# Thirteen weight blocks of a transformer stage formed by single-pass products, with GpSimd making their low parts

## The reference

```python
h = rms_norm_2(x, norm1_g[l]) * (1 + sc1) + sh1
proj = h @ w_in[l]                                   # 1024 -> 7168
ca, cb, q, k, v, gate_conv, gate_attn = jnp.split(proj, offsets, axis=-1)
y_conv = conformer_conv(ca, cb, conv_dw[l], ...)     # u = a*sigmoid(b); 31 taps per channel; layer norm; silu; @ w_pw2
y_attn = diff_attention(q, k, v, cos, sin, ...)      # rms norm of q and k per map, rope, 16 maps, softmax
merged = jax.nn.sigmoid(gate_conv) * y_conv + jax.nn.sigmoid(gate_attn) * y_attn
x = x + g1 * (merged @ w_out[l])
```

## Time and profile before

| | |
|---|---|
| median of 3 runs | 1594.1 us (1593.49 to 1595.61) |
| the profiled execution's own time | 1594.08 us |
| its span in the trace | 1592.4 us |
| mean granted TensorE clock | 0.985 |
| PE, DVE, ACT, POOL busy | 1518.2, 736.5, 490.1, 45.3 us |

### The profile page before, as it was taken

The page is one execution under the profiler, slowest core; times in us unless marked ns, Lnnn a source line. Parts: engine busy times, 40 slices in busy tenths (PEclk is TensorE's granted clock), DMA queues, the critical chain, the costliest instruction groups (busy, mean ns, idle before and its releaser), DMA issues.

```text
span 1592.4 us, 27380 instructions
## 1 busy us (share of the span) xinstructions
PE 1518.2 (95%) x10546; PEld 1015.8 (64%) x10546; DVE 736.5 (46%) x1245; ACT 490.1 (31%) x758; POOL 45.3 (3%) x97
## 2 busy tenths in 40 slices
PE   6999999999999899999999999988989999989988
PEld 6999968757697799997854455463434444444442
DVE  5555447255665565555499855461211221222212
ACT  4433343152443443334001262032222222222221
POOL 6000010100000000001000000000000000000000
PEclk9999999999999999999999999998999999999999
DMA  9855384221346475637644433419997997988984
GB/s 321 287 169 181 136 299 142 89 98 54 124 155 231 146 257 165 210 127 256 204 145 142 171 102 112 170 53 403 348 402 297 360 349 257 346 342 313 352 333 167
DMA packets 156217, 350.92 MB, mean 220 GB/s; under 512 B 12655, under 2 KB 57919, under 8 KB 155712
## 3 DMA queue, kind: packets, MB, share of 16 engines
q1 hardware_dynamic: 152464, 343.05, 59.6%
q0 software_dynamic: 1792, 3.09, 0.7%
q10 hardware_dynamic: 1840, 3.17, 0.5%
HBM read 579.89 MB, written 2.16 MB: 366 GB/s over the span
## 4 chain that ended last, share of the span: by engine, by line
PE 71%; DVE 12%; DMA 8%; SPq 3%; ACT 3%; issue 2%; DVEq 0%; ACTq 0%
PE bank L675 16%; PE bank L2879 8%; PE bank L654 8%; PE bank L2907 6%; DVE arena L2356 6%; PE bank L2157 5%; PE bank L1078 4%; DMA ring<-in_w_exp_down 4%; DMA ring<-in_w_exp_gu 3%; PE bank L2809 3%; PE bank L1814 3%; PE bank L2789 3%; PE bank L1831 2%; SPq L3147 2%; PE bank L1087 2%
## 5 line engine op out<-in xcount | busy, mean ns | idle before, releaser
L675 PE MATMUL bank<-x_high,w_high 128*128 128x256 f32 x704 | 201.1, 286 | 6.1 <-DVEq L252 6.1
L675 PE MATMUL bank<-x_low,w_high 128*128 128x256 f32 x704 | 200.7, 285 | 0.0
L675 PE MATMUL bank<-x_high,w_low 128*128 128x256 f32 x704 | 199.5, 283 | 0.0
L747 DVE TENSOR_TENSOR w_low<-ring,w_high 128x2048 fp32r<-128x2048 f32 x60 | 137.4, 2292 | 76.8 <-ACT w_high L712 76.6
L2157 PE MATMUL bank<-ring,xT 128*128 128x512 f32 x384 | 166.0, 593 | 1.8 <-ACT arena L2514 1.8
L675 PEld LDWEIGHTS bank<-x_high,w_high 128*128 128x128 f32 x704 | 134.0, 190 | 7.6 <-issue 6.9
L675 PEld LDWEIGHTS bank<-x_high,w_low 128*128 128x128 f32 x704 | 135.5, 192 | 0.0
L675 PEld LDWEIGHTS bank<-x_low,w_high 128*128 128x128 f32 x704 | 134.2, 191 | 0.7
L712 ACT ACTIVATE w_high<-ring 128x2048 fp32r<-128x2048 f32 x60 | 114.6, 1913 | 60.4 <-PE bank L654 59.2
L2157 PEld LDWEIGHTS bank<-ring,xT 128*128 128x128 f32 x384 | 72.6, 190 | 91.9 <-issue 91.8
L2907 PE MATMUL bank<-ring,arena 128*32 128x512 f32 x1024 | 118.7, 605 | 7.9 <-DMA ring<-in_w_exp_down 7.9
(11 more groups left out here) (573 smaller groups left out, 2418.8 us busy)
## 6 DMA issues: line engine op xcount, KB each, us to landing
ring<-in_w_exp_gu SPq DMA_DIRECT2D x512, 512.0 KB
ring<-in_w_exp_down SPq DMA_DIRECT2D x128, 1024.0 KB
ring<-in_w_in SPq DMA_DIRECT2D x42, 768.0 KB, 6.1
ring<-in_ffn_w_gate SPq DMA_DIRECT2D x22, 1024.0 KB, 5.8
ring<-in_ffn_w_up SPq DMA_DIRECT2D x22, 1024.0 KB, 8.6
ring<-in_ffn_w_down SPq DMA_DIRECT2D x21, 1024.0 KB, 10.1
ring<-in_w_ada SPq DMA_DIRECT2D x24, 768.0 KB, 5.7
ring<-in_w_in SPq DMA_DIRECT2D x21, 512.0 KB, 7.9
```

Source lines behind the costliest of these rows:

```text
L675: ins = pe.eng.matmul(bank[:, k * S:(k + 1) * S], ff_w[f][w][:, c, k, :], (x_high, x_low)[x][:, c, :], start=c == 0 and i == 0, stop=c == ...
L747: v.eng.tensor_tensor(low[:], raw_piece((base + a) % NS, p), high[:].bitcast(F32), ALU.subtract).then_inc(low_set[p], 1)
```

## The change

Block 0 stays as it was. Blocks 1 to 13 are formed by the three single-pass products, each block in two halves, so there are 26 halves (numbered 0 to 25, block 1 has halves 0 and 1). ScalarE makes all 26 high parts; VectorE makes the low parts of halves 0 and 1, GpSimd those of the other 24. (`BY_VEC` is 2.) High parts rotate over three places in the ring's tails (the last one has its own), so half k is cut after TensorE has left half k-3. The stage's input is cut too: `x_high` and `x_rest`, and again in place after block 0.

The convolution is as it was: its running sum stays in SBUF, and its instructions and operands are unchanged (L2417 in the new file).

Along with it: the squares of q and k are formed and summed on ScalarE (`map_squares`: 64 instructions of 128x64 with an accumulated sum) where VectorE had four of 128x2048; q's norm is applied later, as a scale in the exponentials; both gains are folded on the part that isn't turned; the rope runs over q and k together (12 instructions instead of 24); the convolution's transposes of the second half come after block 11 instead of block 9; the gates' store to DRAM has a place of its own, and VectorE waits for it ahead of the copies of q.

```diff
+            for half in cut_halves[BY_VEC:]:
+                eng.wait_ge(half_high, half.number)
+                eng.tensor_tensor(half.low, half.cut(wide[half.block % NS], half.k),
+                                  half.high.bitcast(F32), ALU.subtract).then_inc(pool_low, 1)
...
+            for k in range(26):
+                block = 1 + k // 2
+                cut_halves.append(Half(first + block,
+                                       by_columns if block < 4 else by_rows, k % 2,
+                                       places[k % 3] if k < 25 else last_place,
+                                       cut_halves[k - 3] if 3 <= k < 25 else None))
...
+            def half_parts(half):
+                k = cut_halves.index(half)
+                if k < BY_VEC:
+                    return pe_half(pe, half)
+                wait(pool_low, k + 1 - BY_VEC)
+                return half.high, half.low
...
+            def split_projected(to, block, x_parts):
+                banks = [to.fill() for _ in range(T)]
+                for m, half in enumerate(cut_halves[2 * block - 2:2 * block]):
+                    high, low = half_parts(half)
+                    for t, b in enumerate(banks):
+                        for c in range(4):
+                            for i, (w, x) in enumerate(PAIRS):
+                                ins = mm(ps[b][:], x_parts[x][:, 4 * m + c, t * P:(t + 1) * P],
+                                         (high, low)[w][:, c, :], start=m == c == i == 0,
+                                         stop=m == 1 and c == 3 and i == 2, skip_group_check=True)
+                        if m:
+                            ins.then_inc(to.full, 1)
+                    half.left_by = (to.full, to.n - (0 if m else T - 1))
...
-            for _ in range(4):
-                projected(to_act)
+            for block in range(4, 8):
+                split_projected(to_act, block, x_parts)
             conv_to_tokens(0)
-            for _ in range(2):
-                projected(to_act)
+            for block in range(8, 12):
+                split_projected(to_act, block, x_parts)
             conv_to_tokens(1)
-            for _ in range(2):
-                projected(to_act)
             wait(qk_ready, 1)
...
+            wait(x_high_now, IN_XN)
+            tt(x_rest[0], xT[:], x_high[:].bitcast(F32), ALU.subtract).then_inc(x_parts_set, 1)
+            for half in cut_halves[:BY_VEC]:
+                vec_half(v, half)
...
-                do(tt(sq, qk[:, at], qk[:, at], ALU.mult))
-                do(e.tensor_reduce(ss[:, at], sq, AX.X, ALU.add))
...
+            def map_squares(i, n, t):
+                for m in range(n * 8, (n + 1) * 8):
+                    ins = f(squares[:, i * T + t, m], qk[:, i * T + t, m], ACT.Square,
+                            accum_out=ss[:, i * T + t, m:m + 1])
+                do(ins)
```

More of the change, by code:

```diff
@@ L2152, in features @@
                 release.append((to.full, to.n))
+            first = pe.block
+            places = [ring_tail[(first + i) % NS] for i in range(3)]
+            x_rest.append(ring_tail[(first + 3) % NS][:].rearrange("p (c s) -> p c s", c=DC))
+            for k in range(26):
[4 more added lines that the diff above has]
+                                       cut_halves[k - 3] if 3 <= k < 25 else None))
@@ new lines, in half_parts, with split_features @@
+            def half_parts(half):
[4 more added lines that the diff above has]
+                return half.high, half.low
+            def split_features(to, block, x_parts):
+                for half in cut_halves[2 * block - 2:2 * block]:
+                    b = to.fill()
+                    high, low = half_parts(half)
+                    for k in range(2):
+                        for c in range(DC):
+                            at = slice(k * P, (k + 1) * P)
+                            for i, (w, x) in enumerate(PAIRS):
+                                ins = mm(ps[b][:, k * S:(k + 1) * S], (high, low)[w][:, c, at],
+                                         x_parts[x][:, c, :], start=c == i == 0,
+                                         stop=c == DC - 1 and i == 2, skip_group_check=True)
+                    ins.then_inc(to.full, 1)
+                    half.left_by = (to.full, to.n)
+                pe.block += 1
+                release.append((to.full, to.n))
@@ L2230, in pe_part @@
             features(to_vec)
-            features(to_act)
+            wait(x_parts_set, OF_HYBRID)
+            split_features(to_act, 1, (x_high, x_rest[0]))
             wait(taps_loaded, 64)
@@ L2367, in vec_part @@
             wait(qk_set, 1)
-            for i in range(2):
-                at = slice(i * T, (i + 1) * T)
-                do(tt(sq, qk[:, at], qk[:, at], ALU.mult))
-                do(e.tensor_reduce(ss[:, at], sq, AX.X, ALU.add))
-            v.ask()
+            do(e.reciprocal(ss, ss))
+            for t in range(T):
+                x = qk[:, T + t]
+                do(tt(x, x, along(ss[:, T + t], HD), ALU.mult))
+                do(tt(x, x, every(kg, MAPS), ALU.mult))
+            for t in range(T):
+                turned = qk[:, t, :, 0:ROT]
+                do(tt(turned, turned, every(qg[:, 0:ROT], MAPS), ALU.mult))
             wait(convT_set, 4)
@@ L2376, in vec_part @@
             v.ask()
[L2377 to L2386, removed]
+            for t in range(T):
+                both = qk[:, t::T]
+                sin, cos = (trig[:, j, t].unsqueeze(1).unsqueeze(1).to_broadcast([P, 2, MAPS, 8])
+                            for j in range(2))
+                at = slice(2 * t, 2 * t + 2)
+                x1, x2 = both[:, :, :, 0:8], both[:, :, :, 8:16]
+                do(tt(rot_a[:, at], x1, sin, ALU.mult))
+                do(tt(rot_b[:, at], x2, sin, ALU.mult))
                 do(tt(x1, x1, cos, ALU.mult))
                 do(tt(x2, x2, cos, ALU.mult))
-                do(tt(x1, x1, rot_b[:, i], ALU.subtract))
-                do(tt(x2, x2, rot_a[:, i], ALU.add))
+                do(tt(x1, x1, rot_b[:, at], ALU.subtract))
+                do(tt(x2, x2, rot_a[:, at], ALU.add))
             e.sem_inc(qk_ready, 1)
+            do(ts(ss[:, 0:T], ss[:, 0:T], HD ** -0.5, None, ALU.mult))
             v.answer()
@@ L2397, in vec_part @@
             e.sem_inc(ln_ready, 1)
+            wait(gate_stored, 32)
             for c in range(0, HEADS, 2):
@@ L2505, in act_part @@
             act_to_features(a, xT, DC, modT[:, 0], modT[:, 1])
+            a.taken()
+            f(x_high[:], xT[:], ACT.Copy).then_inc(x_high_now, 1)
+            for half in cut_halves[0:3]:
+                act_half(a, half)
             a.get()
@@ L2514, in evict, with conv_gate @@
                 do(f(dst, src, how, **more), act_free)
-            for c in range(0, DC, 2):
+            def conv_gate(c):
                 b = mine.take()
@@ L2520, in act_part, with qk_columns @@
                 do.count[act_free.name] = do.count.get(act_free.name, 0) + 1
[L2521 to L2526, removed]
+            def qk_columns(i, n, t):
+                b = mine.take()
+                evict(qk[:, i * T + t, n * 8:(n + 1) * 8, :], view(ps[b], 0, (8, HD)))
+            def map_squares(i, n, t):
[3 more added lines that the diff above has]
+                do(ins)
+            wait(vec_full, 2)
+            wait(x_parts_set, OF_HYBRID)
+            f(x_again[:], xT[:], ACT.Copy).then_inc(x_high_now, 1)
+            conv_gate(0)
+            act_half(a, cut_halves[3])
+            conv_gate(2)
+            for half in cut_halves[4:7]:
+                act_half(a, half)
+            conv_gate(4)
+            act_half(a, cut_halves[7])
+            conv_gate(6)
+            act_half(a, cut_halves[8])
             def conv_tokens(half):
```

104 lines of the change are left out of this document (76 added, 28 removed).

## The result

The changed kernel takes 1677.76 us (median of 4, 1676.35 to 1678.73) beside 1594.7 for the kernel before on the same chip: ratio 1.0526 [1.051, 1.0541], 83 us slower.

What follows compares the result with a forecast made beforehand. Up to 919 us two full queues, TensorE's blocks and VectorE's convolution, bound it. Exclusion moves the convolution's end to 977 and the mask from 928.0 to 996.5: 1594.1 + 68.5 = 1662.6, said as 1662, range 1612 to 1682.

Steps and rivals of the forecast that it cites:

- T: End of the whole convolution on VectorE: forecast at 977 us, from 879.05 + 0.6 + 21 x 4.6 + 1.
- the way from T to the mask: VectorE's norms, passes over k, rope, layer norm and copies between convolution and masked scores: 19.5 us, mask at 996.5.
- TensorE's part: Single-pass products in blocks 1 to 13: 11.52 us a features block, 10.98 a projected one, saving 36.1 us.
- the side-by-side rival: GpSimd's subtractions and VectorE's convolution run together: T = 880, mask at 904, -24 us, 1570; chance 0.08.
- GpSimd's price: One 128x2048 low-part subtraction on GpSimd: 4.6 us, the middle of 4.1 and 5.1.
- Exclusion: Convolution taps and GpSimd subtractions, each reading two SBUF tiles, exclude each other, so their times add: 21 x 4.6 us.
- Exclusion, GpSimd getting its turns: Main case: beside the convolution GpSimd's subtractions each get a turn; 1645 to 1680 us, chance 0.55.
- VectorE holding: Rival: VectorE never lets GpSimd in during the convolution, halves stay 47.5 us, mask at 990, 1656; chance 0.22.
- the rival's sign: Mark of the rival with VectorE holding: TensorE waits for low parts, not for the convolution (`conv_ready`).
- my "1 us" for it: ScalarE's high parts waiting behind bank copies in its queue, blocks 4 to 9: full, not over; counted 1 us.
- Late start of block 1: Block 1 on TensorE waits for two of VectorE's three 2.29 us subtractions: taken as 2 us.
- Behind the mask: Softmax chain on VectorE and ScalarE taken as unchanged; blocks 12 and 13 save 5.8 us in shadow: counted 0.

Runs made afterwards that it cites:

- experiment 9: Experiment 8's kernel with ScalarE's exponential and sine ahead of block 1's high parts, and half 2's high part behind the copy of x: 1578.64 us, 0.9909.
- experiment 3: Kernel before the change plus eight unneeded 128x2048 subtractions on GpSimd beside the convolution's first half: 1630.9 us in one run.
- Experiment 1: Changed kernel with the convolution's running sum in PSUM banks until the last tap, so most taps read one SBUF tile: 1598.7 us, 1.0031.
- experiment 10: Experiment 9's kernel with the convolution's running sum put back in SBUF: 1664.07 us, 1.0453.
- experiments 5 and 6: Kernel before plus unneeded GpSimd subtractions parted by one or two memsets beside the convolution: 1631.37 us; the same with VectorE draining before each tap: 1638.39 us.
- Experiment 2: Changed kernel with VectorE waiting for its own last instruction before the first of each tap's four: 1678.29 us, 1.0522.
- experiment 8: Experiment 1's kernel with GpSimd starting half 22 only behind the passes over k (after the layer norm): 1591.45 us, 0.9986.

## Why the prediction was right, and where its sizes were off

The sign, and the reason for it, were right: 1677.8 measured, 1662 forecast, range 1612 to 1682. The total was 15.8 us short. Two of its terms, T and the way from T to the mask, were each off by more than twice that and nearly cancelled: the mask came 5.2 us later than forecast. Nearly all of the rest is the 5.9 and 4.4 us behind it.

**TensorE's part: right.** 96 products in 11.50 us, four projected blocks in 43.55 and 43.80 (10.9 each, 10.98 forecast); the side-by-side rival's mask at 904, 2 us ahead of what experiment 9 reached once VectorE and the late start of block 1 were out of the way (905.88). **GpSimd's price: right.** 4.49 to 4.93 us up to the convolution's end where it got its turn, 4.6 forecast from four times a smaller tile. The Trainium skill's 4497 ns for an add of 2048 float32 columns (GPSIMD Engine Reference, "Elementwise — side-by-side cycle accounting") agrees with the f32 subtractions of experiment 3, 4514.

**Exclusion: right, shown.** Experiment 1 takes away the second SBUF input and with it 79 us, and experiment 10 puts it back into 9 and loses 85; experiment 3 adds eight subtractions and 36 us. The Trainium skill's rule (SBUF — State Buffer, "Who interferes with whom") agrees in this with every run here. One piece of the prediction's evidence was of another kind: the row at 9.51 that showed VectorE held is a `tensor_scalar` with one SBUF input, so it did not yet show the taps held. Their 4878 ns and experiment 3 do.

**The step that failed: "Exclusion, GpSimd getting its turns", all 21 of them, with "VectorE holding" as a case apart.** It is a mixture. GpSimd got eleven turns and was twice held to the end of VectorE's row. So T was 943.5 and not 977, and TensorE waited 37 us twice for low parts (the rival's sign) and not for the convolution. The kernel after and experiments 5 and 6 show on what it hangs: whether GpSimd had stopped reading for longer than a border between 1.8 and 3.1 us while VectorE's instructions followed without a break. In the kernel after both such pauses end with a high part that stood in ScalarE's queue behind a bank copy, and the copy waited for TensorE (5.50 and 3.17 us). ACT in order of time in the kernel after:

```profile
816.92 0.60 ACT L2581 ACTIVATE arena<-bank 128x512 f32<-128x512 f32 x1 [5.50 <-PE bank L2206]
817.55 1.92 ACT L602 ACTIVATE ring_tail<-ring 128x2048 fp32r<-128x2048 f32 x1
```

So ScalarE was not too slow there: my "1 us" for it was wrong in kind, since the order of its queue, more than its load, made GpSimd pause. Experiment 1 has the same two pauses (3.43 and 4.49 us) and no hold. Experiment 2 shows that, had GpSimd had all its turns, T would have been 985 (my 977 was 8 us low, the drains' own cost among it) and the time the same.

**From T to the mask: 19.5 us forecast, 58.2 measured.** Of these 4.4 pass until the second held subtraction delivers (947.95) and 14.6 until TensorE's block and ScalarE's squares are through (962.54). Then the six passes take 25.1 instead of the 6.3 of my sum: I had let all of the halves 17 to 24 run inside the convolution, and five subtractions ran beside these. Rope and what follows took 14.1, near its 12.6. With T 33.5 us early and this stretch 38.7 longer, the mask came 5.2 us later than forecast, at 1001.7 instead of 996.5. That the sum fitted so well is partly luck.

**Late start of block 1: 2 us forecast, 8.9 measured.** Block 1's products began at 771.80. VectorE stood 11.1 us for ScalarE's tables, and these stood in ScalarE's queue behind the high part of half 2, whose load came at 760.44. I had costed the three subtractions and not what ScalarE's queue holds ahead of them. Reordering the queue is experiment 9: the mask comes 11.4 us earlier than in experiment 8 and the time is 12.8 us less.

**Behind the mask: 0 forecast, +5.9 measured.** Up to 2.9 of it is ScalarE's 32 exponentials, which have a scale for each row now: 492 and 602 ns where the two shapes took 401 and 509 before. Another part is the 5.8 us that blocks 12 and 13 save. TensorE is through sooner and then waits 8.9 us for the values; PE in order of time in the kernel after:

```profile
1050.00 3.78 PE L2272 MATMUL bank<-arena,xT 128*128 128x128 f32 x16 [8.90 <-DVEq L2493]
```

The window of it, columns as above:

```profile
1050.00:1054.00 4.00, 4.00 (x17) 3.91 (x18) 0.00 (x0) 1.28 (x1) 0.00 (x0) 0.50 0.66 240
```

And the same transposes in the kernel before, PE in order of time:

```profile
972.66 2.05 PE L2217 MATMUL bank<-arena,xT 128*128 128x128 f32 x16 [0.25 <-DVEq L2430]
```

The granted clock is 0.50 there, the 1.2 GHz level, after 8.9 us of idling, and the 16 transposes take 3.78 us instead of 2.05: +1.7. The rest, about 1.3, is spread over gaps. **The stage behind: +4.4,** not forecast and not explained; in the profiles of the six other kernels with the changed stage it took 559.8 to 561.3 us, beside 559.8 before.

## What to carry to other kernels

Before work is moved to an idle GpSimd, look at what VectorE does in that stretch: if its instructions read two SBUF tiles and GpSimd's read SBUF, the times add up, and both rows still say "busy". The same held for the `tensor_scalar` of the first tap. A running sum in PSUM takes one of the two tiles away at hardly any cost in the instruction (479 against 478 ns in the kernel before) and, with the two other faults mended, turned a loss of 4.5% into a gain of 0.9% (experiments 10 and 9). And the moved step is only as early as what stands ahead of it in its queue: the order of ScalarE's queue was worth 12.8 us.

## What the runs showed of the hardware

- VectorE's two-tile instructions, sent without a break, keep a reading GpSimd out across instructions: 42.3, 42.5 and 47.96 us for a subtraction of 4.5, and 42.28 and 42.07 in experiment 10. The Trainium skill's rule (SBUF — State Buffer, "Who interferes with whom") speaks of the length of one instruction only. Within a row of taps GpSimd got in after pauses of 1.0 to 1.8 us, and not after 3.1 to 4.2; the border lies between, and a drain every four instructions takes it away (4.66). Pauses of 3.60 us, and of 3.75 in experiment 10, at the very start of VectorE's second row did not lose the turn. Why the chip does so stays open.
- After 8.9 us of idling TensorE's first 96 products of block 1 took 13.05 us at a granted clock of 0.89 (11.50 at 1.00 in experiment 9, where it had not idled).
- An fp32r result written by GpSimd to the half's place costs little, if anything, more than an f32 one: 4490 ns at least and 4629 in the median (experiment 1) beside 4504 and 4514 (experiment 3).
